# A hybrid attention block on one core: the last head's mix tiles without memory, and another order at the head's end

## The chip, the cores and the metric

The kernel runs on one core of a Trainium2 chip. The metric is the device time of one execution in microseconds (us). The engines are called PE (TensorE), ACT (ScalarE), DVE (VectorE), POOL (GpSimd) and SP (SyncE, which here only issues DMAs). Each runs its own instruction stream in program order and waits on semaphores.

## The reference, cut to what matters

One row of 1024 tokens with 1024 features, float32. The input is normalised and projected by one matrix into the queries, keys, values and gates of three head groups: A (sliding window with sinks), B (differential attention) and M (attention to 256 memory tokens).

```python
proj = rmsnorm(x, g_norm) @ w_in                      # 1024 x 4352
b_out = rmsnorm(b_heads, b_subln_g) * (1.0 - lam_init)
gated = concatenate([a_out * silu(ag), b_out * silu(bg), m_out * silu(mg)])
y = rmsnorm(x + gated @ w_out, g_final)               # w_out 1536 x 1024
```

## The kernel before, in words

**Numbers.** Every large matrix product is made of three float32r products: each operand is split into a high part (a rounding copy, made on ACT: w_hi, p_hi, mix_hi, wo hi) and a low part (the rest, raw minus high: w_lo, p_lo, mix_lo, wo lo). So a projection or an output product is three matmuls (lines 1282 to 1284).

**Heads.** A loop runs four times, once for each head. In a head, PE projects eight weight tiles w = 0..7 in two halves s (512 tokens each), and each half in four quarters q of six matmuls. Tile 7 is the B gate. Between the quarters, PE does the attention pieces that the table `BETWEEN[(w, s, q)]` names. All engines walk the same list `HEAD`; for each step each of them does its own part, in list order. An `evacuate(w, s)` step follows the last quarter of a half and comes ahead of the pieces that BETWEEN names there. PE takes nothing out of order: if the piece after a quarter must wait, all later quarters wait too.

**The pieces that the change touches**, for head h:
- `b_squares(s)`: the row sums for B's norm. POOL squares b_out (L856) and later subtracts (L859), ACT copies the high part between the two (L709), PE multiplies by ones (L1509, L1510), DVE scales the result (L1183). ACT's copy goes to a slot of p_hi, a ring of two slots that the steps b_spread, m_spread and b_squares use in list order (`PT_AT`); it waits until the user two places back has been consumed by PE (`p_slot_free`).
- `b_finish(s)`: ACT takes a square root (L715), DVE a reciprocal of 128x512 (L1189) and a product into b_out (L1191).
- `b_gate`: DVE multiplies b_out into the B gate, two halves (L1199). It needs both b_finish and the evacuated gate (L1056).
- `a_spread(3)`, `a_mix(3)`: PE transposes probabilities (L1489), DVE copies them (L1175), PE multiplies by the values (L1500), DVE gates the result (L1116). `m_spread`, `m_mix` are the same for M; the mix output has one bank (mixo), so each mix waits until DVE's gate (L1116) of the one before has read it (o_free).
- `m_norm(m)`: ACT takes the exponentials (L693, L695), DVE a reciprocal (L1137), POOL a product (L836).

**The tail.** `mixed` in device memory holds 12 tiles of 128 rows x 1024 tokens, three for each head. Each head spills its three gate buffers there, and after the heads they come back as mix_raw by row tiles of 128 tokens. The last head's tiles 9 to 11 make that trip at the end of the heads (`spill(g, H)`, `load_mix(.., 1)`). ACT makes mix_hi and the high parts of the output weights wo 1..11, POOL makes mix_lo and the low parts of wo 1 and 2 (`POOL_WO`), DVE those of wo 3 to 11 and one piece of mix_lo. PE's output products then run over eight row tiles x two halves x 12 tiles; for the first pair of row tiles it goes j = 0..6 for all four outputs, and then j = 7..11 one output at a time, because these weights come last. Weights 4 to 11 lie over the normalised input, so they are loaded when the last projection is done.

Of the kernel before, what the change touches and what calls it, by code (L numbers as in the profile page):

```python
# [20 lines left out]
F32 = mybir.dt.float32  # L21
F32R = mybir.dt.float32r
ALU = mybir.AluOpType
# [3 lines left out]
P = 128  # L27
# [6 lines left out]
HEADS = 4  # L34
DK = 64
AQ, AK, AV, AG, BQ, BK, BV, BG, MQ, MG = 0, 512, 640, 768, 1280, 1792, 2304, 2816, 3328, 3840
MIX_TILES = 12
POOL_WO = 2
LAM_INIT = 0.8 - 0.6
# [42 lines left out]
    (7, 0, 1): [("a_mix", 2), ("m_norm", 3), ("m_spread", 2)],  # L82
    (7, 0, 2): [("m_mix", 1)],
    (7, 0, 3): [("m_spread", 3), ("m_mix", 2)],
    (7, 1, 0): [("a_spread", 3), ("m_mix", 3), ("b_squares", 1)],
    (7, 1, 1): [("b_finish", 0)],
    (7, 1, 2): [("b_finish", 1)],
    (7, 1, 3): [("b_gate",), ("a_mix", 3)],
}
# [73 lines left out]
def build(nc, x, mem, w_in, g_norm, a_sinks, lq1, lk1, lq2, lk2, subln_g, g_mem, w_mem_kv, w_out,  # L163
          g_final, y):
    mixed = nc.dram_tensor("mixed", (MIX_TILES * P, SEQ), F32).ap()

# [24 lines left out]
    with ctx:  # L191
        def sem(name):
# [5 lines left out]
        w_lo = sb("w_lo", [P, 2, KT * P], F32R)  # L198
        gates = {g: sb(f"gate_{g}", [P, SEQ]) for g in "abm"}
        ident = sb("ident", [P, P])  # L200
# [79 lines left out]
        MIX = MIX_TILES * P * 4  # L280
        spread_end = begins["mk_raw"] + 2 * HEADS * MEM * 4
        mix_raw = [sb_over("mix_raw0", [P, MIX_TILES, P], spread_end - MIX, spread_end),
                   sb_over("mix_raw1", [P, MIX_TILES, P], begins["b_bias"], main_end)]
        mix_hi = [sb_over("mix_hi0", [P, MIX_TILES, P], main_end, nc.sbuf_usable_end, F32R),
# [76 lines left out]
        mix_full = [sem("mix_full0"), sem("mix_full1")]  # L361
        mix_last = [sem("mix_last0"), sem("mix_last1")]
        wo_full = [sem(f"wo_full{j}") for j in range(1, MIX_TILES)]
        wo_hi_done = sem("wo_hi_done")
        wo_lo_first = sem("wo_lo_first")
        wo_lo_done = sem("wo_lo_done")
# [26 lines left out]
        def _(sp):  # L393
# [75 lines left out]

            def load_mix(par, t, part):  # L470

                js, done = ((slice(0, 9), mix_full), (slice(9, 12), mix_last))[part]
                sp.dma_start(mix_raw[par][:, js, :], mixed_v[:, js, bass.ds(t * P, P)]).then_inc(done[par], 16)

# [8 lines left out]
            sp.wait_ge(mkv_lo, 2 * HEADS)  # L483
            load_mix(0, 0, 0)
# [3 lines left out]
            load_mix(1, 1, 0)  # L488
            sp.wait_ge(s_full, NS * HEADS)
# [3 lines left out]
            sp.wait_ge(acc_full, PRE_ACC + 2 * NT * HEADS)  # L493
            for j in range(4, 8):
                load_wo(j)
            for g in "mab":
                spill(g, H)
            load_wo(8)
            load_wo(9)
            for g in "mab":  # L500
                sp.wait_ge(spilled[g], 16 * HEADS)
            load_mix(0, 0, 1)
            load_mix(1, 1, 1)
            for j in range(10, MIX_TILES):
                load_wo(j)
# [15 lines left out]
            def next_pair(z, split):  # L521

                for par in range(2):
                    sp.wait_ge(mix_lo_done, split[par])
                    for part in range(2):
                        load_mix(par, z * 2 + (par + 2), part)
# [5 lines left out]
            sp.wait_ge(mix_lo_mid, 1)  # L532
            next_pair(0, (4, 5))
            with sp.Fori(0, ST // 2 - 2) as n:
                next_pair(n + 1, (n * 4 + 7, n * 4 + 9))
            for par in range(2):
# [6 lines left out]
        def _(act):  # L543
# [195 lines left out]

            def mix_hi_part(par, js, arrived, full):  # L740
                act.wait_ge(arrived[par], full)
                act.activation(mix_hi[par][:, js, :], mix_raw[par][:, js, :], ACT.Copy).then_inc(mix_hi_done, 1)  # L742

            def wo_hi_part(j):
                act.wait_ge(wo_full[j - 1], 32)
                act.activation(wo[j - 1][:, 0, :], wo_raw[j - 1][:, :], ACT.Copy).then_inc(wo_hi_done, 1)

            mix_hi_part(0, slice(0, 3), mix_full, 16)
            act.wait_ge(t_full, at(T_AT[("b_spread", 3, 3)], HEADS - 1, NTB, PRE_T))
            mix_hi_part(1, slice(0, 3), mix_full, 16)  # L750
            wo_hi_part(1)
            wo_hi_part(2)
            mix_hi_part(0, slice(3, 9), mix_full, 16)
            mix_hi_part(1, slice(3, 9), mix_full, 16)
# [18 lines left out]
            with act.Fori(0, ST // 2 - 1) as z:  # L773
                for par in range(2):

                    act.wait_ge(y_full, z * 4 + 2 * (par + 1))
                    mix_hi_part(par, slice(0, 9), mix_full, z * 16 + 32)
                    mix_hi_part(par, slice(9, 12), mix_last, z * 16 + 32)
                    finish_row(par, z)
# [5 lines left out]
        def _(pool):  # L785
# [91 lines left out]
            def mix_lo_part(par, js, n):  # L877
# [3 lines left out]
                                   ALU.subtract).then_inc(mix_lo_done, 1)  # L881

            pool.wait_ge(pt_done, NMIX * HEADS)
            pool.wait_ge(t_full, PRE_T + NTB * HEADS)
            for par in range(2):
                mix_lo_part(par, slice(0, 3), par)
            for j in range(1, POOL_WO + 1):
                pool.wait_ge(wo_hi_done, j)
                pool.tensor_tensor(wo[j - 1][:, 1, :], wo_raw[j - 1][:, :], wo[j - 1][:, 0, :].bitcast(F32),
                                   ALU.subtract).then_inc(wo_lo_first, 1)  # L890
            mix_lo_part(1, slice(3, 9), 3)
            for par in range(2):
                mix_lo_part(par, slice(9, 12), 4 + par)
            with pool.Fori(0, ST // 2 - 1) as z:
                for par in range(2):
                    for p, js in enumerate((slice(0, 9), slice(9, 12))):
                        mix_lo_part(par, js, z * 4 + (6 + 2 * par + p))


        @block.vector  # L900
        def _(dve):
# [106 lines left out]
            with dve.Fori(0, HEADS) as h:  # L1008
# [194 lines left out]
                for s in HEAD:  # L1203
# [40 lines left out]
            dve.tensor_tensor(mix_lo[0][:, 3:9, :], mix_raw[0][:, 3:9, :], mix_hi[0][:, 3:9, :].bitcast(F32),  # L1244
                              ALU.subtract).then_inc(mix_lo_mid, 1)
# [33 lines left out]
        def _(pe):  # L1279
# [269 lines left out]
            def w_out_ready(j):  # L1549
                if j == 0:  # L1550
                    pe.wait_ge(w_lo_done, PRE_TILES + NT * HEADS + 1)
                elif j <= POOL_WO:
                    pe.wait_ge(wo_lo_first, j)
                else:
                    pe.wait_ge(wo_lo_done, j - POOL_WO)

# [4 lines left out]
            for j in range(7):  # L1561
                w_out_ready(j)
                for par in range(2):
                    if j == 0:
                        pe.wait_ge(mix_lo_done, 1 + par)
                    if j == 3:
                        pe.wait_ge(*((mix_lo_done, 3) if par else (mix_lo_mid, 1)))
                    for s in range(2):
                        y_product(par, s, j)
            for par in range(2):  # L1570
                pe.wait_ge(mix_lo_done, 4 + par)
                for s in range(2):
                    for j in range(7, MIX_TILES):
                        w_out_ready(j)
                        last = y_product(par, s, j)
                    last.then_inc(y_full, 1)
            with pe.Fori(0, ST // 2 - 1) as z:
                for par in range(2):
                    pe.wait_ge(mix_lo_done, z * 4 + (7 + 2 * par))
# [27 lines left out]
```

## Time and profile before

| | us |
|---|---|
| median of 3 runs | 776.75 |
| lowest and highest run | 775.76, 778.9 |
| the profiled execution: span from first to last instruction | 775.9 |
| PE busy in it | 755.9 (97%) |
| DVE, ACT, POOL busy | 433.7, 321.7, 236.4 |

The profiled execution has no separate time of its own beside its span of 775.9 us; what lies around the span is in the 0.85 us up to the median. Times in the rows are microseconds from the start of the span. Matmul ends are modelled: of two dense matmuls the second starts 0.23 us after the first although each is shown 0.39 us long.

### The profile page before, as it was taken

The page shows a single profiled execution, that of the slowest core. Times are in us where ns is not written, and L with a number is a line of the kernel's source. Part 1 is how long each engine was busy: PE and PEld are TensorE (multiplying, and loading weights), DVE is VectorE, ACT ScalarE, POOL GpSimd, SP SyncE. Part 2 cuts the span into 40 slices and gives each one's busy share as a digit, 9 for nine tenths or more (in the row PEclk, how much of TensorE's full clock was granted, in tenths as well). Part 3 has the DMA queues.
Part 4 walks back from the last instruction along what each step waited for, and adds up shares of the span by engine and source line. Part 5 has one row for each costly group of instructions (what it writes and reads, how often), then busy time and mean ns, then how long its engine had stood idle before and what let it go on. Part 6 is the DMA issues. An engine that isn't in the chain of part 4 may idle for free.

```text
span 775.9 us, 12264 instructions
## 1 busy us (share of the span) xinstructions
PE 755.9 (97%) x3908; PEld 596.3 (77%) x3908; DVE 433.7 (56%) x915; ACT 321.7 (41%) x727; POOL 236.4 (30%) x204
## 2 busy tenths in 40 slices
PE   7999999999999999999999999999999988999996
PEld 7887877778877777887777688877768866888885
DVE  5875235666763566677346666734666695422231
ACT  5761323444542344454334444433444472421220
POOL 3663212224422222442322244222224451311110
PEclk9999999999999999999999999999999999999998
DMA  7662120011042001103300110240011359554111
GB/s 251 209 171 55 28 54 29 28 28 29 1 136 54 27 27 27 27 0 121 70 27 27 27 27 0 91 100 27 27 41 44 85 135 279 162 150 124 65 54 54
DMA packets 83155, 56.61 MB, mean 73 GB/s; under 512 B 36400, under 2 KB 75312, under 8 KB 83120
## 3 DMA queue, kind: packets, MB, share of 16 engines
q1 hardware_dynamic: 83120, 56.25, 26.0%
q8 instruction: 10, 0.16, 0.1%
q14 instruction: 25, 0.20, 0.1%
HBM read 45.75 MB, written 10.49 MB: 72 GB/s over the span
## 4 chain that ended last, share of the span: by engine, by line
PE 88%; issue 4%; DVE 2%; POOL 2%; DMA 2%; SPq 1%; ACT 0%; DVEq 0%; POOLq 0%
PE acc L1282 17%; PE acc L1284 16%; PE acc L1283 16%; PE score L1403 5%; PE score L1401 4%; PE score L1282 3%; PE score L1283 3%; PE score L1284 3%; PE trans L1422 2%; PE trans L1282 2%; PE trans L1284 2%; PE trans L1283 2%; POOL w_lo L803 2%; PE mixo L1282 2%; PE score L1479 2%
## 5 line engine op out<-in xcount | busy, mean ns | idle before, releaser
L1282 PE MATMUL acc<-x_hi,w_hi 128*128 128x512 f32 x544 | 221.4, 407 | 0.2 <-POOL w_lo L803 0.2
L1283 PE MATMUL acc<-x_lo,w_hi 128*128 128x512 f32 x544 | 214.6, 395 | 0.0
L1284 PE MATMUL acc<-x_hi,w_lo 128*128 128x512 f32 x544 | 214.6, 394 | 0.0
L803 POOL TENSOR_TENSOR w_lo<-w_raw,w_hi 128x512 fp32r<-128x512 f32 x86 | 114.1, 1348 | 205.5 <-ACT w_hi L548 205.5
L1282 PEld LDWEIGHTS acc<-x_hi,w_hi 128*128 128x128 f32 x544 | 102.1, 188 | 27.6 <-issue 5.7
L1284 PEld LDWEIGHTS acc<-x_hi,w_lo 128*128 128x128 f32 x544 | 102.0, 188 | 24.9
L1283 PEld LDWEIGHTS acc<-x_lo,w_hi 128*128 128x128 f32 x544 | 102.2, 188 | 20.0
L1077 DVE CUSTOM_DVE_ANT_0 logits<-score,b_bias 128x512 f32<-128x512 f32 (+1 forms) x96 | 57.2, 602 | 44.6 <-PE score L1403 34.9
L653 ACT ACTIVATE logits<-logits,stats_b 128x256 f32<-128x256 f32 (+3 forms) x64 | 52.7, 825 | 68.7 <-DVE stats_b L1085 68.7
L662 ACT ACTIVATE p_hi<-trans 128x512 fp32r<-128x512 f32 x56 | 32.6, 596 | 74.2 <-PE trans L1422 44.1
L548 ACT ACTIVATE w_hi<-w_raw 128x512 fp32r<-128x512 f32 x86 | 49.4, 624 | 26.2 <-PE acc L1284 20.4
L830 POOL TENSOR_SCALAR logits<-logits,stats_b,small 128x256 f32<-128x256 f32 (+3 forms) x32 | 28.3, 883 | 104.2 <-DVE stats_b L1094 104.2
L1104 DVE TENSOR_TENSOR p_lo<-trans,p_hi 128x512 fp32r<-128x512 f32 x56 | 37.9, 689 | 31.4 <-ACT p_hi L662 31.0
L880 POOL TENSOR_TENSOR mix_lo<-mix_raw,mix_hi 128x384 fp32r<-128x384 f32 (+2 forms) x17 | 28.2, 1677 | 85.4 <-ACT mix_hi L742 85.4
L1097 DVE SCALAR_TENSOR_TENSOR logits<-logits,stats_b 128x256 f32<-128x256 f32 (+3 forms) x32 | 28.3, 885 | 38.0 <-POOL logits L830 38.0
L701 ACT ACTIVATE a_band<-a_band,stats_a 128x128 f32<-128x128 f32 x64 | 25.0, 393 | 58.1 <-DVE stats_a L1162 58.1
L1403 PE MATMUL score<-k_lo,q_b 64*128 64x512 f32 (+1 forms) x96 | 43.9, 457 | 0.0
L1401 PE MATMUL score<-k_b,q_b 128*128 128x512 f32 (+1 forms) x96 | 40.1, 418 | 0.0
L1282 PE MATMUL score<-wo,mix_hi 128*128 128x512 f32 x88 | 35.4, 403 | 4.1 <-DVE wo L1248 3.8
L1403 PEld LDWEIGHTS score<-k_lo,q_b 64*128 64x128 f32 x96 | 17.5, 183 | 22.9 <-issue 20.3
L1283 PE MATMUL score<-wo,mix_hi 128*128 128x512 f32 x88 | 34.8, 395 | 0.0
L1284 PE MATMUL score<-wo,mix_lo 128*128 128x512 f32 x88 | 34.8, 395 | 0.0
(193 smaller groups left out, 1333.7 us busy)
## 6 DMA issues: line engine op xcount, KB each, us to landing
w_raw<-in_w_in SPq DMA_DIRECT2D x68, 256.0 KB, 3.4
wo_raw<-in_w_out SPq DMA_DIRECT2D x22, 256.0 KB, 5.6
mix_raw<-mixed SPq DMA_DIRECT2D x8, 576.0 KB, 5.8
w_raw<-in_w_mem_kv SPq DMA_DIRECT2D x16, 256.0 KB, 3.9
logits<-in_x SPq DMA_DIRECT2D x8, 512.0 KB, 4.5
x_res<-in_x SPq DMA_DIRECT2D x8, 512.0 KB, 3.3
out_y<-y_row SPq DMA_DIRECT2D x16, 256.0 KB, 2.1
mixed<-gate_a SPq DMA_DIRECT2D x4, 512.0 KB, 3.1
```

The lines of the kernel that those rows point to most:

```text
L548: act.activation(w_hi[:, slot, cols], w_raw[:, slot, cols], ACT.Copy).then_inc(w_hi_done, 1)
L653: act.activation(logits[:, i % 2, c, 0:width], logits[:, i % 2, c, 0:width], ACT.Exp, bias=b_neg[:, 2 * (i % 2) + c:2 * (i % 2) + c + 1], ...
L662: act.activation(out, trans[:, bank, :], ACT.Copy).then_inc(t_hi, 1)
L803: last = pool.tensor_tensor(w_lo[:, slot, cols], w_raw[:, slot, cols], w_hi[:, slot, cols].bitcast(F32), ALU.subtract)
L830: pool.tensor_scalar(logits[:, i % 2, 1, 0:width], logits[:, i % 2, 1, 0:width], b_inv[:, 2 * (i % 2) + 1:2 * (i % 2) + 2], neg_lam, ALU.m ...
L1077: dve.tensor_tensor_reduce(out=logits[:, i % 2, c, a:a + n], in0=score[:, unit % S_RING, 0:n], in1=b_bias[:, rel:rel + n], scale=1.0, scal ...
L1104: dve.tensor_tensor(out, trans[:, T_AT[step] % T_RING, :], hi.bitcast(F32), ALU.subtract)\
L1282: pe.matmul(out, a_hi, b_hi, start=start, stop=False, skip_group_check=True)
L1283: pe.matmul(out, a_hi, b_lo, start=False, stop=False, skip_group_check=True)
L1284: return pe.matmul(out, a_lo, b_hi, start=False, stop=stop, skip_group_check=True)
L1401: pe.matmul(out, q_b[:, c, rows_i], k_b[:, c, a:a + n], start=True, stop=False, skip_group_check=True)
L1403: pe.matmul(out, q_b[ps, c, rows_i], k_lo[ps, a:a + n], start=False, stop=True, skip_group_check=True).then_inc(s_full, 1)
```

## The change

1. The last head's mix tiles (9 to 11) are split into mix_hi and mix_lo straight from the gate buffers on chip, for every row tile. Their spill and the loads of that part go away; `mixed` has nine tiles.
2. All eleven low output weights are made by DVE; POOL makes none. DVE also makes both middle pieces of mix_lo, after wo 2.
3. In every head: b_squares(1) moves from after the quarter (7,1,0) to after (7,0,2); b_finish(0) from (7,1,1) to (7,0,3); b_finish(1) from (7,1,2) to (7,1,1); a_mix(3) from after (7,1,3) to after (7,1,2), and so ahead of the evacuation of the last half and of b_gate.
4. After the last projection SP issues weights 4 to 11 in one row, with no spill or load between.

```diff
-POOL_WO = 2
+SPILL_TILES = 9
-    (7, 0, 2): [("m_mix", 1)],
-    (7, 0, 3): [("m_spread", 3), ("m_mix", 2)],
-    (7, 1, 0): [("a_spread", 3), ("m_mix", 3), ("b_squares", 1)],
-    (7, 1, 1): [("b_finish", 0)],
-    (7, 1, 2): [("b_finish", 1)],
-    (7, 1, 3): [("b_gate",), ("a_mix", 3)],
+    (7, 0, 2): [("m_mix", 1), ("b_squares", 1)],
+    (7, 0, 3): [("m_spread", 3), ("m_mix", 2), ("b_finish", 0)],
+    (7, 1, 0): [("a_spread", 3), ("m_mix", 3)],
+    (7, 1, 1): [("b_finish", 1)],
+    (7, 1, 2): [("a_mix", 3)],
+    (7, 1, 3): [("b_gate",)],
...
-            for j in range(4, 8):
-                load_wo(j)
-            for g in "mab":
-                spill(g, H)
-            load_wo(8)
-            load_wo(9)
-            for g in "mab":
-                sp.wait_ge(spilled[g], 16 * HEADS)
-            load_mix(0, 0, 1)
-            load_mix(1, 1, 1)
-            for j in range(10, MIX_TILES):
+            for j in range(4, MIX_TILES):
                 load_wo(j)
...
+            def gates_hi_part(par, t):
+                act.activation(mix_hi[par][:, SPILL_TILES:MIX_TILES, :], gate_rows[:, :, bass.ds(t * P, P)], ACT.Copy)\
+                   .then_inc(mix_hi_done, 1)
...
-            mix_hi_part(0, slice(9, 12), mix_last, 16)
-            mix_hi_part(1, slice(9, 12), mix_last, 16)
+            act.wait_ge(o_free, NO * HEADS)
+            act.wait_ge(b_gated, 2 * HEADS)
+            gates_hi_part(0, 0)
+            gates_hi_part(1, 1)
...
+            def gates_lo_part(par, t, n):
+
+                pool.wait_ge(mix_hi_done, n + 1)
+                js = slice(SPILL_TILES, MIX_TILES)
+                pool.tensor_tensor(mix_lo[par][:, js, :], gate_rows[:, :, bass.ds(t * P, P)],
+                                   mix_hi[par][:, js, :].bitcast(F32), ALU.subtract).then_inc(mix_lo_done, 1)
...
-            for j in range(1, POOL_WO + 1):
-                pool.wait_ge(wo_hi_done, j)
-                pool.tensor_tensor(wo[j - 1][:, 1, :], wo_raw[j - 1][:, :], wo[j - 1][:, 0, :].bitcast(F32),
-                                   ALU.subtract).then_inc(wo_lo_first, 1)
-            mix_lo_part(1, slice(3, 9), 3)
             for par in range(2):
-                mix_lo_part(par, slice(9, 12), 4 + par)
+                gates_lo_part(par, par, 4 + par)
...
-            dve.wait_ge(mix_hi_done, 3)
...
-            for j in range(POOL_WO + 1, MIX_TILES):
+            for j in range(1, MIX_TILES):
                 dve.wait_ge(wo_hi_done, j)
                 dve.tensor_tensor(wo[j - 1][:, 1, :], wo_raw[j - 1][:, :],
                                   wo[j - 1][:, 0, :].bitcast(F32), ALU.subtract).then_inc(wo_lo_done, 1)
+                if j == 2:
+                    for par in range(2):
+                        dve.wait_ge(mix_hi_done, 3 + par)
+                        dve.tensor_tensor(mix_lo[par][:, 3:9, :], mix_raw[par][:, 3:9, :],
+                                          mix_hi[par][:, 3:9, :].bitcast(F32), ALU.subtract).then_inc(mix_lo_mid, 1)
```

## Rows read from the trace of the kernel before

**Rows 1.** Timeline of PE, last head, tile 7: start us, us, engine, line, operation.

```profile
618.25 0.28 PE L1284 MATMUL mixo<-p_hi,mv_lo 128*128 128x256 f32 x1
618.37 0.39 PE L1282 MATMUL acc<-x_hi,w_hi 128*128 128x512 f32 x1
...
620.79 0.28 PE L1284 MATMUL mixo<-p_hi,mv_lo 128*128 128x256 f32 x1
...
622.67 0.36 PE L1282 MATMUL mixo<-p_hi,mv_hi 128*128 128x256 f32 x1
...
623.46 0.39 PE L1509 MATMUL trans<-p_hi,ones 128*128 128x512 f32 x1
```

**Rows 2.** Timeline of ACT in the same stretch.

```profile
616.45 0.47 ACT L693 ACTIVATE m_probs<-score,stats_m 128x256 f32<-128x256 f32 x1 [2.24 <-PE trans L1458]
...
621.10 0.63 ACT L709 ACTIVATE p_hi<-logits 128x512 fp32r<-128x512 f32 x1
621.75 1.28 ACT L715 ACT_TABLE_LOAD   x1
623.05 0.64 ACT L715 ACTIVATE logits<-logits 128x512 f32<-128x512 f32 x1
```

**Rows 3.** Timeline of POOL in the same stretch.

```profile
617.75 1.04 POOL L836 TENSOR_TENSOR m_probs<-m_probs,stats_m 128x512 f32<-128x512 f32 x1 [1.25 <-DVE stats_m L1137]
618.75 1.04 POOL L856 TENSOR_TENSOR logits<-b_out 128x512 f32<-128x512 f32 x1
621.81 1.28 POOL L859 TENSOR_TENSOR p_lo<-logits,p_hi 128x512 fp32r<-128x512 f32 x1 [2.02 <-ACT p_hi L709]
```

**Rows 4.** Timeline of DVE, last head's end.

```profile
621.20 0.68 DVE L1104 TENSOR_TENSOR p_lo<-trans,p_hi 128x512 fp32r<-128x512 f32 x1
621.80 0.42 DVE L1116 SCALAR_TENSOR_TENSOR gate_m<-mixo,gate_m 128x256 f32<-128x256 f32 x1
622.95 0.69 DVE L1175 COPY a_pt<-trans 128x512 f32<-128x512 f32 x1 [0.73 <-PE trans L1489]
...
624.73 3.34 DVE L1189 RECIPROCAL logits<-logits 128x512 f32<-128x512 f32 x1
628.11 0.69 DVE L1191 TENSOR_TENSOR b_out<-b_out,logits 128x512 f32<-128x512 f32 x1
...
632.10 2.30 DVE L1191 TENSOR_TENSOR b_out<-b_out,logits 128x512 f32<-128x512 f32 x1
```

**Rows 5.** Timeline of POOL near the end of the head before.

```profile
481.14 1.04 POOL L856 TENSOR_TENSOR logits<-b_out 128x512 f32<-128x512 f32 x1
```

**Rows 6.** Timeline of ACT and PE, from the last projection on.

```profile
628.22 0.69 PE L1500 MATMUL mixo<-a_pt,a_v 128*64 128x64 f32 x16
...
628.33 0.60 ACT L645 ACTIVATE gate_b<-acc 128x512 f32<-128x512 f32 x1 [1.54 <-PE acc L1284]
...
630.64 0.47 PE L1282 MATMUL score<-w_hi,mix_hi 128*128 128x512 f32 x1 [1.74 <-POOL mix_lo L880]
```

**Rows 7.** Timeline of PE in the tail.

```profile
641.86 0.59 PE L1282 MATMUL score<-wo,mix_hi 128*128 128x512 f32 x1 [2.13 <-DVE wo L1248]
...
645.61 0.39 PE L1282 MATMUL trans<-wo,mix_hi 128*128 128x512 f32 x1
```

**Rows 8.** Windows: us, PE, PEld, DVE, ACT, POOL busy (instructions), PEclk, DMA, GB/s.

```profile
630.00:640.00 10.00, 8.86 (x36) 6.52 (x36) 9.97 (x7) 7.14 (x8) 8.92 (x5) 1.00 1.03 254
643.00:644.00 1.00, 1.00 (x4) 0.71 (x4) 1.00 (x2) 0.00 (x0) 0.00 (x0) 0.50 0.70 209
```

**Rows 9.** Timeline of PE in the prologue.

```profile
13.58 1.62 PE L1290 MATMUL trans<-ident,logits 128*128 128x128 f32 x8 [2.40 <-DVE k_b L940]
```

**Rows 10.** The chain that ended last, in the tail.

```profile
687.84 0.23 PE trans L1282
...
769.48 0.24 PE trans L1284
```

**Rows 11.** Line 1248, DVE's low output weights.

```profile
L1248 DVE TENSOR_TENSOR wo<-wo_raw,wo x9: 1211/1221/1226, 640.6 to 659.0; 128x1024 fp32r<-128x1024 f32 x9
```

More of the change, by code:

```diff
@@ L164, in build @@
           g_final, y):
-    mixed = nc.dram_tensor("mixed", (MIX_TILES * P, SEQ), F32).ap()
+    mixed = nc.dram_tensor("mixed", (SPILL_TILES * P, SEQ), F32).ap()
     x_rows = x.rearrange("b (t p) d -> p (b t) d", p=P)
@@ L198, in build @@
         w_lo = sb("w_lo", [P, 2, KT * P], F32R)
-        gates = {g: sb(f"gate_{g}", [P, SEQ]) for g in "abm"}
+        gate_rows = sb("gates", [P, 3, SEQ])
+        gates = {g: gate_rows[:, n, :] for n, g in enumerate("abm")}
         ident = sb("ident", [P, P])
@@ L280, in build @@
         MIX = MIX_TILES * P * 4
+        MIX_RAW = SPILL_TILES * P * 4
         spread_end = begins["mk_raw"] + 2 * HEADS * MEM * 4
-        mix_raw = [sb_over("mix_raw0", [P, MIX_TILES, P], spread_end - MIX, spread_end),
-                   sb_over("mix_raw1", [P, MIX_TILES, P], begins["b_bias"], main_end)]
+        mix_raw = [sb_over("mix_raw0", [P, SPILL_TILES, P], spread_end - MIX_RAW, spread_end),
+                   sb_over("mix_raw1", [P, SPILL_TILES, P], begins["b_bias"], main_end)]
         mix_hi = [sb_over("mix_hi0", [P, MIX_TILES, P], main_end, nc.sbuf_usable_end, F32R),
@@ L361, in build @@
         mix_full = [sem("mix_full0"), sem("mix_full1")]
-        mix_last = [sem("mix_last0"), sem("mix_last1")]
         wo_full = [sem(f"wo_full{j}") for j in range(1, MIX_TILES)]
         wo_hi_done = sem("wo_hi_done")
-        wo_lo_first = sem("wo_lo_first")
         wo_lo_done = sem("wo_lo_done")
@@ L468, in load_wo, with load_mix @@
                       .then_inc(wo_full[j - 1] if j else raw_full[0], 16)
-            def load_mix(par, t, part):
-                js, done = ((slice(0, 9), mix_full), (slice(9, 12), mix_last))[part]
-                sp.dma_start(mix_raw[par][:, js, :], mixed_v[:, js, bass.ds(t * P, P)]).then_inc(done[par], 16)
+            def load_mix(par, t):
+                sp.dma_start(mix_raw[par][:, :, :], mixed_v[:, :, bass.ds(t * P, P)]).then_inc(mix_full[par], 16)
             def load_residual(par, t):
@@ L483, in _ @@
             sp.wait_ge(mkv_lo, 2 * HEADS)
-            load_mix(0, 0, 0)
+            load_mix(0, 0)
             sp.wait_ge(s_full, at(S_AT[("b", 7, 1, 1)], H, NS))
@@ L487, in _ @@
             sp.wait_ge(s_free_dve, len(S_BY_DVE) * HEADS)
-            load_mix(1, 1, 0)
+            load_mix(1, 1)
             sp.wait_ge(s_full, NS * HEADS)
@@ L524, in next_pair @@
                     sp.wait_ge(mix_lo_done, split[par])
-                    for part in range(2):
-                        load_mix(par, z * 2 + (par + 2), part)
+                    load_mix(par, z * 2 + (par + 2))
                 for par in range(2):
@@ L530, in next_pair @@
                     store(par, z)
-            sp.wait_ge(mix_lo_mid, 1)
-            next_pair(0, (4, 5))
+            sp.wait_ge(mix_lo_mid, 2)
+            next_pair(0, (1, 2))
             with sp.Fori(0, ST // 2 - 2) as n:
-                next_pair(n + 1, (n * 4 + 7, n * 4 + 9))
+                next_pair(n + 1, (n * 4 + 5, n * 4 + 7))
             for par in range(2):
@@ L737, in _, with mix_hi_part @@
                         b_finish(s[1])
-            def mix_hi_part(par, js, arrived, full):
-                act.wait_ge(arrived[par], full)
+            def mix_hi_part(par, js, full):
+                act.wait_ge(mix_full[par], full)
                 act.activation(mix_hi[par][:, js, :], mix_raw[par][:, js, :], ACT.Copy).then_inc(mix_hi_done, 1)
+            def gates_hi_part(par, t):
+                act.activation(mix_hi[par][:, SPILL_TILES:MIX_TILES, :], gate_rows[:, :, bass.ds(t * P, P)], ACT.Copy)\
+                   .then_inc(mix_hi_done, 1)
             def wo_hi_part(j):
@@ L746, in wo_hi_part @@
                 act.activation(wo[j - 1][:, 0, :], wo_raw[j - 1][:, :], ACT.Copy).then_inc(wo_hi_done, 1)
-            mix_hi_part(0, slice(0, 3), mix_full, 16)
+            mix_hi_part(0, slice(0, 3), 16)
             act.wait_ge(t_full, at(T_AT[("b_spread", 3, 3)], HEADS - 1, NTB, PRE_T))
-            mix_hi_part(1, slice(0, 3), mix_full, 16)
+            mix_hi_part(1, slice(0, 3), 16)
             wo_hi_part(1)
             wo_hi_part(2)
-            mix_hi_part(0, slice(3, 9), mix_full, 16)
-            mix_hi_part(1, slice(3, 9), mix_full, 16)
+            mix_hi_part(0, slice(3, 9), 16)
+            mix_hi_part(1, slice(3, 9), 16)
             for j in range(3, 7):
                 wo_hi_part(j)
-            mix_hi_part(0, slice(9, 12), mix_last, 16)
-            mix_hi_part(1, slice(9, 12), mix_last, 16)
+            act.wait_ge(o_free, NO * HEADS)
+            act.wait_ge(b_gated, 2 * HEADS)
+            gates_hi_part(0, 0)
+            gates_hi_part(1, 1)
             for j in range(7, MIX_TILES):
@@ L776, in _ @@
                     act.wait_ge(y_full, z * 4 + 2 * (par + 1))
-                    mix_hi_part(par, slice(0, 9), mix_full, z * 16 + 32)
-                    mix_hi_part(par, slice(9, 12), mix_last, z * 16 + 32)
+                    mix_hi_part(par, slice(0, 9), z * 16 + 32)
+                    gates_hi_part(par, z * 2 + (par + 2))
                     finish_row(par, z)
@@ L886, in _ @@
                 mix_lo_part(par, slice(0, 3), par)
-            for j in range(1, POOL_WO + 1):
-                pool.wait_ge(wo_hi_done, j)
-                pool.tensor_tensor(wo[j - 1][:, 1, :], wo_raw[j - 1][:, :], wo[j - 1][:, 0, :].bitcast(F32),
-                                   ALU.subtract).then_inc(wo_lo_first, 1)
-            mix_lo_part(1, slice(3, 9), 3)
             for par in range(2):
-                mix_lo_part(par, slice(9, 12), 4 + par)
+                gates_lo_part(par, par, 4 + par)
             with pool.Fori(0, ST // 2 - 1) as z:
                 for par in range(2):
-                    for p, js in enumerate((slice(0, 9), slice(9, 12))):
-                        mix_lo_part(par, js, z * 4 + (6 + 2 * par + p))
+                    mix_lo_part(par, slice(0, 9), z * 4 + (6 + 2 * par))
+                    gates_lo_part(par, z * 2 + (par + 2), z * 4 + (7 + 2 * par))
         @block.vector
@@ L1239, in _ @@
                         b_gate()
-            dve.wait_ge(mix_hi_done, 3)
             dve.wait_ge(pt_done, NMIX * HEADS)
             dve.wait_ge(t_full, PRE_T + NTB * HEADS)
-            dve.tensor_tensor(mix_lo[0][:, 3:9, :], mix_raw[0][:, 3:9, :], mix_hi[0][:, 3:9, :].bitcast(F32),
-                              ALU.subtract).then_inc(mix_lo_mid, 1)
-            for j in range(POOL_WO + 1, MIX_TILES):
+            for j in range(1, MIX_TILES):
                 dve.wait_ge(wo_hi_done, j)
@@ L1551, in w_out_ready @@
                     pe.wait_ge(w_lo_done, PRE_TILES + NT * HEADS + 1)
-                elif j <= POOL_WO:
-                    pe.wait_ge(wo_lo_first, j)
                 else:
-                    pe.wait_ge(wo_lo_done, j - POOL_WO)
+                    pe.wait_ge(wo_lo_done, j)
             pe.wait_ge(t_free, PRE_T + NTB * HEADS)
@@ L1566, in _ @@
                     if j == 3:
-                        pe.wait_ge(*((mix_lo_done, 3) if par else (mix_lo_mid, 1)))
+                        pe.wait_ge(mix_lo_mid, 1 + par)
                     for s in range(2):
@@ L1570, in _ @@
             for par in range(2):
-                pe.wait_ge(mix_lo_done, 4 + par)
+                pe.wait_ge(mix_lo_done, 3 + par)
                 for s in range(2):
@@ L1578, in _ @@
                 for par in range(2):
-                    pe.wait_ge(mix_lo_done, z * 4 + (7 + 2 * par))
+                    pe.wait_ge(mix_lo_done, z * 4 + (6 + 2 * par))
                     for s in range(2):
```

## The prediction

> **What bounds the kernel now.** I read the page first: the span is 775.9 us (in the table above, with the page's busy times), and PE is busy for 97% of it. So only what makes PE wait, or what lets it wait less, moves the time. Then I read the timelines of the four engines at the end of the last head and in the tail. Through the end of a head PE never stops: its matmuls follow each other 0.23 us (512 columns) or 0.12 us (256 columns) apart [rows 1]. In the tail it does stop. The chain of the tail has PE from 687.84 to 769.48 + 0.24, which is 81.9 us for ten of the sixteen output units, 8.19 us each [rows 10]. Sixteen would be 131.0 us, but the first output product starts at 630.64 [rows 6] and the last ends at 769.7, 139.1 us. So 8.0 us of the tail are waits and a slow clock. That is all that parts 1, 2 and 4 of the change can win there.
>
> **The head's end, step by step.** I take the last head's times; the others have the same pattern (POOL's square of b_out stands at 618.75 here and at 481.14 one head earlier, one head period apart) [rows 3, 5].
>
> First wait: b_squares(1) now follows m_mix(1) directly. PE would issue it at 618.37, where the next quarter starts now [rows 1]. Its operands come by a chain that doesn't get earlier: m_spread(2) frees m_probs, ACT's exponentials of m_norm(3) start at 616.45 [rows 2], POOL's product follows at 617.75 and POOL's square, behind it in POOL's order, at 618.75 for 1.04 us, to 619.8 [rows 3]. Then ACT's high copy, 0.63 [rows 2], and POOL's subtraction, 1.28 [rows 3], with about 0.05 to 0.15 between engines: 0.08 is what lies between 621.10 + 0.63 and 621.81. So PE can start at 619.79 + 0.06 + 0.63 + 0.08 + 1.28 + 0.15 = 621.99. It waits 3.6 us. Before, ACT's copy came at 621.10, POOL ended at 623.09, and PE asked for it at 623.46 [rows 1 to 3]: the quarter, a_spread(3) and m_mix(3) covered the chain. In the new order nothing covers it, and everything behind it in PE's queue waits too.
>
> Second wait, small: b_squares takes two matmuls, 0.46. The quarter (7,0,3) starts at 622.45, and the last matmul of m_mix(2) at 622.45 + 2.42 = 624.87 (618.37 to 620.79 before [rows 1]), ending at 625.15. With b_squares(1) ahead of it in the ring, the user of p_hi two places before m_spread(3) is m_spread(2) now, not m_spread(1). So ACT's copy for m_spread(3), which ran ahead of m_mix(2) before, waits for the end of m_mix(2), and behind it on ACT wait the table load and the square root. Copy (0.6, as in L709) to 625.8, DVE's low part and gate (0.1 + 0.6 + 0.42 with the spacing of [rows 4]) to 626.85. PE wants m_mix(3) 1.88 after the last matmul of m_mix(2) [rows 1], at 626.75: 0.2 us of wait.
>
> Third wait: b_finish(0) now stands on DVE ahead of the copy for a_spread(3) and of the gate of m_mix(3), and PE's a_mix(3) needs both. ACT: copy to 625.77, table load and square root 1.96 (621.75 to 623.05 + 0.64) to 627.73 [rows 2]. DVE: reciprocal from 627.78, product 3.38 later, copy 0.61 later, gate 0.71 later, 0.42 long (624.73 to 628.11 and the durations beside it) [rows 4]: 632.9. PE is ready for a_mix(3) at 626.94 + 0.79 (622.67 to 623.46 [rows 1]) + twelve matmuls 2.8 + 0.1 = 630.6, and starts at 633.0: 2.4 us.
>
> The second square root needs no new table and is long done; the second reciprocal comes only behind the gate of m_mix(3), so a_mix(3) doesn't wait for it.
>
> Together 3.6 + 0.2 + 2.4 = 6.2 us in each head. After the first three heads nothing gives it back, since PE has no wait there now: 18.6 us. The next head's evacuations don't suffer: DVE is done with b_gate 5 us after PE starts the next head, before the first half of it ends at 24 x 0.23 = 5.6 us.
>
> At this place a rule of the Trainium skill speaks for more. The row shows the table load with 1.28 us, the square root 0.02 behind it, and the copy before it ended 0.02 ahead [rows 2]. "ScalarE: Activation LUTs", section "What ACT_TABLE_LOAD costs", adds a drain of 1.38 us to each load, 2.66 in all. By that the third wait would be 1.4 longer in each head. The row shows no such drain.
>
> SP issues the spills of heads 0 to 2 behind the moved gates; the waits of its queue lie beside 137.6 us of head (618.75 - 481.14), and what it loads next is needed one tile later, 11 us of PE, so I cost that at nothing.
>
> **The last head and the tail.** Parts 1 and 4: the spills and the late loads go. PE's (7,1,3) is issued by 633.0 + 0.61 + 1.40 = 635.0. ACT's tanh stands 0.2 behind it, and the first output product 2.31 behind that (628.33 to 630.64 [rows 6]): 637.5, against 630.64, so 6.9 late; a_mix no longer fills that gap. Weights 4 to 11 are eight tiles of 512 KB. At the 254 GB/s of the window 630 to 640, where the queue is full [rows 8], they take 16.5 us, to about 654; PE wants tile 11 some 96 matmuls x 0.23 = 22 us after its start, at 659.6. That is cover of some 5 us, so the DMA queue and ACT (idle otherwise) cost nothing; without that cover it would be 2.1 us for a tile. The gates' splits on ACT and POOL replace equal ones from mix_raw. DVE: its second reciprocal runs 632.9 to 636.3, then 0.69, the gate of A, the last evacuation and two products of b_gate. These have two inputs in SBUF, as the one of L1191 that took 2.30 beside POOL's wo work instead of 0.69 [rows 4]; now POOL has only the two small mix_lo pieces, so I give them 0.4 us of waiting and DVE is free near 639.7. Low weight 1 takes 1.22 [rows 11], to 640.9, and PE wants it at 640.4: a wait of 0.7. All later ones come at 1.2 or less on DVE against 2.8 us of PE for each j. So of the 8.0 us of loss about 0.4 + 0.7 stay: 6.9 - 8.0 + 1.1 = 0.0. The tail pays for its own late start and no more.
>
> **The clock.** At 641.86, after 2.13 us of waiting, the matmuls take 0.63 and the window behind has a granted clock of 0.50 (1.2 GHz) [rows 7, 8]; the same shows behind a 2.40 wait in the prologue, where eight transposes take 1.62 [rows 9]. The wait of 1.74 at 630.64 did no such thing [rows 6]. The first of these cost 1.7 us: the nine matmuls that start from 641.86 on, up to the one at 645.61 [rows 7], take 3.75 us, and dense ones 9 x 0.23 = 2.07. The new kernel has four waits of 3.6, four of 2.4 and one of 2.3. None falling gives 0, all nine give 15.3. I take five to six, 9 us, as every 3.6 should do it, and the others in part.
>
> **The sum.** 776.75 + 18.6 + 0.0 + 9 = 804. The span of 775.9 belongs to an execution at the median or just below it (0.85 apart), so the difference goes onto the median.
>
> **Rivals.**
> - Only the first wait is real, and the reciprocals are hidden: 3 x 3.8, the tail 2.4 better, the clock 4 x 1.7: 776.75 + 11.4 - 2.4 + 6.8 = 793. For it: a_mix(3) has 12 matmuls of cover. Against: the DVE chain is 7.8 us long. Chance 0.05.
> - Faster: PE finds b_squares(1) ready. It decides at 618.37: if POOL's subtraction has ended by then, the reciprocals start 3 to 4 us earlier too, no head waits, and only the tail counts, 0.6 - 8.0 + 1.1 = -6.3: 770.4. Against: POOL's square starts only at 618.75 [rows 3]. Chance 0.05.
> - The third wait is longer by the drain that the Trainium skill's ScalarE page gives: 4 x 1.4 more, 776.75 + 18.6 + 5.5 + 9 = 810. The row of the table load speaks against it: chance 0.02.
> - The tail fails: weights 4 to 11 come in slower than 2.8 us a tile, or DVE's eleven low weights become the bound. Two tiles late, 4 us: 808. Chance 0.03.
>
> **How the numbers follow.** The forecast has 0.85. Its range is 776.75 + 18.6 = 795 without any fall of the clock and 811 with all nine; with 1 us for the engine spacings, and reaching to the first rival, 793 to 813. Less than 0.5% (3.9 us) is about what a measurement here can't tell from no change. Faster: the second rival, 0.05. Same: a part of the waits hidden by something that I don't see and the tail's gain against the rest, 0.02. Slower 0.93.
>
> **What would show it.** In each head a wait of PE for POOL L859 of some 3.6 us ahead of b_squares(1), and one for DVE L1116 or L1175 of some 2.4 ahead of the last a_mix; a head period 6 to 9 us longer; first output product some 2.3 us behind tanh; no waits of PE on wo after the first; PEclk below 1 at the heads' ends. The prediction is wrong if PE shows no wait ahead of b_squares(1), or if the clock stays at 1.00 there (then 795).

## The result and the profile after

The changed kernel takes 807.69 us (median of 4 runs, 803.77 to 808.52) against 776.52: a ratio of 1.0385, 95% interval 1.0361 to 1.0408. It is slower by 31 us. The forecast was 804, 793 to 813. In the runs with both on record the time is 1.75 to 1.95 us above the span. So the profile of the kernel before, with its span of 775.9, is of an execution of about 777.7, 1.2 above the median, and the spans differ by 29.7 where the medians differ by 31.2.

The page of the kernel after, its head and the two rows of shares over time:

```profile
span 805.6 us, 12254 instructions
...
PE 764.2 (95%) x3908; PEld 602.9 (75%) x3908; DVE 434.9 (54%) x918; ACT 321.6 (40%) x727; POOL 232.9 (29%) x201
...
PE   6899999999799999988999998899999969999996
...
PEclk9999999999999999989999999999999988999999
```

PE had been busy for 97% of a span of 775.9. A slice is 20.1 us. PE's row has its dips where the heads end (slices 11, 18 and 19, 25 and 26, 33, counted from 1; those at 2 and 40 are the prologue and the end), and the clock's row is 8 at the second head's end (18) and at the last one's (33 and 34). It stays at 9 elsewhere: the third head's slow stretch (501.03 to some 507) lies across two slices, and the first head's is short (210.1 to 213.6).

Who PE waited for in the kernel after (us in total, times, longest):

```profile
PE trans L1507 <- POOL p_lo L853: 13.9, 4, 3.5
PE mixo L1498 <- DVE gates L1112: 8.6, 4, 2.2
...
PE score L1280 <- POOL mix_lo L874: 2.4, 1, 2.4
```

The first two are new: four times 3.5 us in front of b_squares(1) (now L1507), four times 2.2 in front of a_mix(3) (now L1498). The waits for the output weights, 3.8 us in five parts in the kernel before, are gone from the list. In the timeline of PE, head 1 of the kernel after:

```profile
350.77 0.28 PE L1282 MATMUL mixo<-p_hi,mv_lo 128*128 128x256 f32 x1
354.53 0.76 PE L1507 MATMUL trans<-p_hi,ones 128*128 128x512 f32 x1 [3.49 <-POOL p_lo L853]
355.10 0.63 PE L1508 MATMUL trans<-p_lo,ones 128*128 128x512 f32 x1
...
368.25 0.69 PE L1498 MATMUL mixo<-a_pt,a_v 128*64 128x64 f32 x16 [2.16 <-DVE gates L1112]
```

Compare [rows 1], where the last matmul of m_mix(1) at 618.25 is followed 0.12 us later by the next quarter. Here 3.76 us lie between. Behind the gap matmuls start 0.43 us apart; a window of it (columns as in [rows 8]) has the granted clock at 0.50, that is the lower of its two levels, 1.2 GHz:

```profile
355.00:356.00 1.00, 1.00 (x4) 0.71 (x3) 0.24 (x1) 0.00 (x0) 0.00 (x0) 0.50 0.00 0
```

The chain that the prediction wrote down stands in the timelines of POOL and ACT at the last head's end, kernel after:

```profile
643.27 1.04 POOL L830 TENSOR_TENSOR m_probs<-m_probs,stats_m 128x512 f32<-128x512 f32 x1 [1.26 <-DVE stats_m L1133]
644.26 1.04 POOL L850 TENSOR_TENSOR logits<-b_out 128x512 f32<-128x512 f32 x1
646.12 1.26 POOL L853 TENSOR_TENSOR p_lo<-logits,p_hi 128x512 fp32r<-128x512 f32 x1 [0.82 <-ACT p_hi L697]
```

```profile
645.42 0.63 ACT L697 ACTIVATE p_hi<-logits 128x512 fp32r<-128x512 f32 x1 [1.94 <-POOL logits L850]
...
652.27 0.60 ACT L650 ACTIVATE p_hi<-trans 128x512 fp32r<-128x512 f32 x1 [0.63 <-PE mixo L1282]
652.89 1.28 ACT L703 ACT_TABLE_LOAD   x1
654.18 1.15 ACT L703 ACTIVATE logits<-logits 128x512 f32<-128x512 f32 x2
```

Product, square, ACT's copy, POOL's subtraction, one behind the other, with 0.1 us between engines. Each of them waits for the one before. The second fence also has the head of the second chain: ACT's copy for m_spread(3) waits for m_mix(2), then the table, then the square roots. And on DVE, in the kernel after, the first reciprocal stands in front of the copy and the gate that PE needs (before they came first, [rows 4]):

```profile
654.85 3.35 DVE L1185 RECIPROCAL logits<-logits 128x512 f32<-128x512 f32 x1 [0.93 <-ACT logits L703]
658.23 0.69 DVE L1187 TENSOR_TENSOR b_out<-b_out,logits 128x512 f32<-128x512 f32 x1
658.84 0.68 DVE L1171 COPY a_pt<-trans 128x512 f32<-128x512 f32 x1
659.45 0.41 DVE L1112 SCALAR_TENSOR_TENSOR gates<-mixo,gates 128x256 f32<-128x256 f32 x1
```

The span grew by 29.7 us. b_squares(1) starts at 209.10, 354.53, 501.03 and 647.53 in the four heads: periods of 145.4, 146.5 and 146.5 against 137.6 before, 25.6 in three heads. The other 4.1 are the fourth head's end and the tail taken together: the first output product comes at 665.77 instead of 630.64, and from there to the end of the last one it takes 133.7 us instead of 139.1.

### The profile page after: what moved, and what is told of

The parts are those of the page before. It is cut to its first block, busy times and chain, and to the rows that moved or that the text cites. A ratio compares the mean times of both kernels' runs of the same rounds, so it can differ in the third digit from the quotient of the medians.

```text
span 805.6 us, 12254 instructions
## 1 busy us (share of the span) xinstructions
PE 764.2 (95%) x3908; PEld 602.9 (75%) x3908; DVE 434.9 (54%) x918; ACT 321.6 (40%) x727; POOL 232.9 (29%) x201
## 4 chain that ended last, share of the span: by engine, by line
PE 81%; issue 6%; POOL 5%; DVE 4%; ACT 2%; DMA 1%; SPq 0%; DVEq 0%; POOLq 0%; ACTq 0%
PE acc L1280 15%; PE acc L1282 14%; PE acc L1281 14%; PE score L1401 5%; PE score L1399 4%; PE score L1280 3%; POOL w_lo L797 3%; PE score L1282 3%; PE score L1281 3%; PE trans L1280 3%; PE trans L1281 3%; PE trans L1282 3%; PE trans L1420 2%; PE score L1477 2%; DVE logits L1185 2%
## 5 line engine op out<-in xcount | busy, mean ns | idle before, releaser
L1280 PE MATMUL acc<-x_hi,w_hi 128*128 128x512 f32 x544 | 223.8, 411 | 0.5 <-POOL w_lo L797 0.5
L874 POOL TENSOR_TENSOR mix_lo<-mix_raw,mix_hi 128x1152 fp32r<-128x1152 f32 (+1 forms) x8 | 18.5, 2317 | 88.0 <-ACT mix_hi L730 88.0
L1280 PE MATMUL trans<-wo,mix_hi 128*128 128x512 f32 x88 | 34.3, 390 | 0.0
```

The lines of the kernel that those rows point to most:

```text
L1280: pe.matmul(out, a_hi, b_hi, start=start, stop=False, skip_group_check=True)
```

## The experiments

Each kernel is an edit of the changed kernel or of the one before, and its ratio is to the kernel before, run beside it on the same chip. e1 to e4 ran on one chip, e5 to e8 on a second, e9 and e10 on a third, and the kernel before had medians of 777.63, 777.78 and 776.87 there, so differences between medians of different chips are good to about 1 us only.

**e1: b_squares(1) alone put back.**

```diff
-    (7, 0, 2): [("m_mix", 1), ("b_squares", 1)],
+    (7, 0, 2): [("m_mix", 1)],
...
-    (7, 1, 0): [("a_spread", 3), ("m_mix", 3)],
+    (7, 1, 0): [("a_spread", 3), ("m_mix", 3), ("b_squares", 1)],
```

> The changed kernel with b_squares(1) back behind m_mix(3) in (7,1,0); all else as changed. Two-waits theory: the wait of 3.5 us at b_squares(1) in each head becomes about 1.6 (ACT's high copy now stands behind the table load and the square root of b_finish(0)), a_mix(3) no longer waits because PE arrives later than the gate of m_mix(3), and the clock stays up in the heads: three heads x 1.6 = 4.8, the tail 4 us better than before: 777, with up to two drops of the clock 780. Rival, that the early b_finish(0) alone costs about as much as b_squares(1): 790 or more.

777.87 us, ratio 0.9999 (0.9986 to 1.0013). Its list of what PE waited for:

```profile
PE trans L1507 <- POOL p_lo L853: 5.5, 4, 1.4
```

No wait for DVE in front of a_mix(3) any more, and a head period of 139.2 (b_squares(1) at 351.54 and 490.75): 1.6 us longer than before, as expected. One step put back in place wins 30 us, and what it leaves is just eaten up by the better tail.

**e2: b_finish(0) and (1) alone put back.**

```diff
-    (7, 0, 3): [("m_spread", 3), ("m_mix", 2), ("b_finish", 0)],
+    (7, 0, 3): [("m_spread", 3), ("m_mix", 2)],
...
-    (7, 1, 1): [("b_finish", 1)],
-    (7, 1, 2): [("a_mix", 3)],
+    (7, 1, 1): [("b_finish", 0)],
+    (7, 1, 2): [("b_finish", 1), ("a_mix", 3)],
```

> The changed kernel with b_finish(0) and b_finish(1) back in (7,1,1) and (7,1,2), b_squares(1) still behind m_mix(1). Two-waits theory: the wait at b_squares(1) stays at 3.5 us with its slow clock (2 to 2.8 us a head), the wait of a_mix(3) goes: three heads x 6 = 18, the tail about 1 us better than before: 792 to 796. Rival, that b_squares(1) is the single cause and the other wait only follows from it: 805 to 808, as the changed kernel.

797.58 us, ratio 1.0243 (1.0202 to 1.0285); 1.6 above the range given. The wait in front of b_squares(1) is as long as in the changed kernel and the one in front of a_mix(3) is gone:

```profile
PE trans L1507 <- POOL p_lo L853: 13.9, 4, 3.5
PE score L1280 <- POOL mix_lo L874: 2.4, 1, 2.4
```

So there are two separate causes: 10 to 11 us of the 31 (by the medians and by the ratios) hang on the two b_finish steps and go without touching b_squares(1). They were moved together; that it is b_finish(0) is read from DVE's rows above, where its reciprocal and product alone stand ahead of the copy and the gate. The two parts don't simply add up. In e1, ACT's copy for m_spread(3) is not held by m_mix(2), so DVE's first reciprocal starts at 627.99, 2 us ahead of b_squares(1) at 629.97, and a_mix(3) finds its operands ready.

**e3: the tail of the changed kernel, the head's end as before.** The six lines of BETWEEN are those of the kernel before.

> The changed kernel with the order of the head's end as before; only the tail differs (gates split on chip, all low weights on VectorE, weights 4 to 11 in one row). Two-waits theory: heads as before with no wait of PE, the tail loses 3.3 us instead of 8 (0.4 at the first product, 2.9 at j = 1, because DVE reaches the low weights late), 772, with one drop of the clock 773.5. Rival, that the change of the tail itself costs time (DMA in one row, gates' splits, DVE as the bound): 777 or more.

772.82 us, ratio 0.9948 (0.9929 to 0.9966). The new tail is a gain of 4.0 us by the ratio. Its profile is of its slowest run (776.75). It shows the wait that is left at j = 1, and the slow clock behind it:

```profile
638.84 0.79 PE L1280 MATMUL score<-wo,mix_hi 128*128 128x512 f32 x1 [2.56 <-DVE wo L1241]
639.43 0.63 PE L1281 MATMUL score<-wo,mix_hi 128*128 128x512 f32 x1
```

**e4: the new order in the kernel before, the old tail.** Only BETWEEN is changed.

> The kernel before with only the new order of the head's end; the tail goes through memory as before. Two-waits theory: the same waits of 3.5 and 2.2 us in each head as the changed kernel, and the old tail's last gap partly hidden since its first output product comes late: 805 to 812. Rival, that the loss is in the new tail: 777 to 790.

814.08 us, ratio 1.0477 (1.0441 to 1.0513): the highest of all, and 2 us above the range given. Its list has the same two waits, 13.9 and 8.6 us, and the old tail's trip through memory still costs a gap at j = 7:

```profile
690.27 0.47 PE L1282 MATMUL score<-wo,mix_hi 128*128 128x512 f32 x1 [2.42 <-DVE wo L1248]
```

e3 and e4 together are the change: 0.9948 x 1.0477 = 1.0423, against 1.0385 measured. The order of the head's end is the whole loss. Behind it the new tail is worth more than in e3, 0.9% instead of 0.5%. The old tail's gap at j = 7 was 1.14 us in the kernel before and is 2.42 here.

**e5: the waits filled with dummy work.** The question was what the slow clock adds to the waits.

```diff
+                    if s == 1:
+                        for _ in range(30):
+                            pe.transpose(out[:, 0:P], ident[:, :], ident[:, :])
                     pe.wait_ge(squares_split, at(s, h, 2))
...
+                    if m == 3:
+                        for _ in range(18):
+                            pe.transpose(trans[:, T_AT[("m_spread", 3)] % T_RING, 0:P], ident[:, :], ident[:, :])
                     out = o_bank(("a_mix", m))
```

> The changed kernel with dummy transposes on PE inside its two waits: 30 ahead of b_squares(1), 18 ahead of a_mix(3), into a bank that is free then, 0.11 us each, so that they end before the waits do. The waits themselves keep their length. Theory that the slow clock adds to the waits: the granted clock stays at 1.00 in the heads, a head's period falls from 146.5 to 143.6 or so, and only the wait at the first output product can still slow the clock: 795 to 799. Rival, that the clock is an accompaniment that costs nothing since PE waits anyway: 806 to 809, as the changed kernel.

796.07 us, ratio 1.0235 (1.0208 to 1.0261). There is more work on PE, and the time is 11.6 us below the changed kernel. The window over head 1, first of the kernel after, then of e5:

```profile
330.00:470.00 140.00, 134.33 (x684) 102.94 (x682) 79.02 (x172) 56.73 (x133) 40.84 (x38) 0.98 0.14 38
```

```profile
330.00:470.00 140.00, 139.61 (x745) 108.19 (x745) 82.04 (x180) 56.62 (x134) 40.62 (x37) 1.00 0.15 41
```

And a_mix(3) in two heads of e5, 143.83 us apart:

```profile
364.09 0.69 PE L1501 MATMUL mixo<-a_pt,a_v 128*64 128x64 f32 x16 [0.20 <-DVE gates L1112]
...
507.92 0.69 PE L1501 MATMUL mixo<-a_pt,a_v 128*64 128x64 f32 x16 [0.20 <-DVE gates L1112]
```

At a full clock a head is 143.8 - 137.6 = 6.2 us longer. That is the waits alone: the dummies did not lengthen them, since b_squares(1) starts 3.69 behind the last matmul of m_mix(1) (349.29 to 352.98) and 3.76 without them. The fourth head and the first output product of e5:

```profile
640.63 0.50 PE L1513 MATMUL trans<-p_hi,ones 128*128 128x512 f32 x1
...
656.60 0.47 PE L1280 MATMUL score<-w_hi,mix_hi 128*128 128x512 f32 x1 [2.58 <-POOL mix_lo L874]
...
659.84 0.50 PE L1280 MATMUL score<-wo,mix_hi 128*128 128x512 f32 x1 [0.20 <-DVE wo L1241]
```

**e6: POOL's square early.** Only POOL's order is changed: the square for b_squares(1) ahead of the product of m_norm(3).

```diff
                 def m_norm(m):
+                    if m == 3:
+                        b_square_made(1)
                     pool.wait_ge(m_inv_made, at(m, h, 4))
...
```

> The changed kernel with POOL's square for b_squares(1) ahead of its product of m_norm(3) instead of behind it. The theory names the chain that makes the first wait (POOL's m_norm(3) product, POOL's square, ACT's copy, POOL's subtraction). With the square made early, the copy waits for m_mix(1) alone (end of it 0.3 us behind the asking), then 0.63 + 0.08 + 1.28 + 0.15: the wait at b_squares(1) falls from 3.5 to 2.3 us, the one of a_mix(3) stays at 2.2: 4.8 us less in four heads, with less of the slow clock 797 to 803. Rival, that the two-slot ring of p_hi sets the wait, not POOL's order: it stays at 3.5, 807.

798.92 us, ratio 1.026 (1.0237 to 1.0283). The two lines of its list:

```profile
PE mixo L1505 <- DVE gates L1119: 8.6, 4, 2.2
PE trans L1514 <- POOL p_lo L860: 8.6, 4, 2.1
```

The first wait falls from 3.5 to 2.1, the second stays. So POOL's order sets the length of the first wait as the prediction had it, down to where the ring takes over: ACT's copy now starts at 642.39, right behind the end of m_mix(1) (642.07 + 0.28).

**e7 and e10: POOL makes one low weight again.** From e3; e10 is the same kernel once more, beside e9.

```diff
+            pool.wait_ge(wo_hi_done, 1)
+            pool.tensor_tensor(wo[0][:, 1, :], wo_raw[0][:, :], wo[0][:, 0, :].bitcast(F32),
+                               ALU.subtract).then_inc(wo_lo_first, 1)
...
-            for j in range(1, MIX_TILES):
+            for j in range(2, MIX_TILES):
...
-                if j == 2:
-                    for par in range(2):
-                        dve.wait_ge(mix_hi_done, 3 + par)
+                if j in (2, 3):
+                    par = j - 2
+                    dve.wait_ge(mix_hi_done, 3 + par)
...
```

> The tail-only kernel (head's end as before) with two edits: POOL makes the low part of weight 1 again, and DVE makes weight 3 between its two pieces of mix_lo. The tail-only kernel waits 2.6 us for DVE's weight 1 and has a slow clock behind it. If DVE's late arrival is the bound of the new tail: a wait of 0.4 at j = 1 and 1.1 at j = 2, no slow clock, 2 to 3 us below the tail-only kernel: 770. If POOL's work slows DVE's products by more than it saves: 773 or more.

> The kernel of e7 once more, beside e9 on the same chip: 771.6 as before, since nothing is changed in it. A theory that e7's gain over the kernel before came from that chip or call expects a ratio nearer to 1 than 0.9916.

771.61 us, ratio 0.9916 (0.9894 to 0.9937), and 771.36, ratio 0.9932 (0.9918 to 0.9946). It is faster than the kernel before by 0.7 to 0.8%. Against e3 it is 1.2 to 1.5 us by the medians and 1.2 to 2.5 by the ratios, where 2 to 3 was expected, and the intervals of the ratios overlap, so that gain is not settled. e3's wait of 2.56 is gone, but in the profile of e7 (an execution of 774.03) the clock fell behind the wait of the first output product instead:

```profile
633.12 0.54 PE L1284 MATMUL score<-w_hi,mix_hi 128*128 128x512 f32 x1 [1.74 <-POOL mix_lo L875]
633.46 0.63 PE L1285 MATMUL score<-w_lo,mix_hi 128*128 128x512 f32 x1
```

**e8: only the gates' tiles split on chip.** Tail of e3 with the low weights made as before (POOL 1 and 2, DVE 3 to 11).

```diff
+            for j in range(1, 3):
+                pool.wait_ge(wo_hi_done, j)
+                pool.tensor_tensor(wo[j - 1][:, 1, :], wo_raw[j - 1][:, :], wo[j - 1][:, 0, :].bitcast(F32),
+                                   ALU.subtract).then_inc(wo_lo_first, 1)
+            mix_lo_part(1, slice(3, 9), 3)
...
```

> Only part 1 of the change (the last head's tiles split from the gate buffers on chip, weights 4 to 11 in one row); the head's end and who makes which low weight as before. By the account of the tail: the gap of 1.3 us at j = 7 and the four of 0.4 behind it go, the wait of 2.1 at j = 3 and the slow clock behind it stay: 3.1 to 3.4 us below the kernel before, 773 to 774. Rival, that the move of the low weights to DVE brings a good part of the tail's gain: 776.

774.99 us, ratio 0.996 (0.9943 to 0.9977): 1 us above the range given. Rows of its timelines of DVE and of POOL show why DVE is late there:

```profile
634.78 4.57 DVE L1201 SCALAR_TENSOR_TENSOR gates<-b_out,small,gates 128x512 f32<-128x512 f32 x2
```

```profile
633.65 2.88 POOL L891 TENSOR_TENSOR wo<-wo_raw,wo 128x1024 fp32r<-128x1024 f32 x1
636.47 2.32 POOL L875 TENSOR_TENSOR mix_lo<-mix_raw,mix_hi 128x768 fp32r<-128x768 f32 x1
640.31 3.04 POOL L882 TENSOR_TENSOR mix_lo<-gates,mix_hi 128x384 fp32r<-128x384 f32 x2 [1.52 <-ACT mix_hi L734]
```

The same two products of b_gate take 1.40 in e7, where POOL is idle by then, and 4.55 in the kernel before, which has the same low weights on POOL. And with the gates' split at 640.31, DVE's next weight is late too. It takes 2.02 instead of the 1.21 of [rows 11]:

```profile
640.47 2.02 DVE L1250 TENSOR_TENSOR wo<-wo_raw,wo 128x1024 fp32r<-128x1024 f32 x1
```

PE's wait at j = 3 is 2.93, longer by the same 0.8 than the 2.13 of [rows 7].

**e9: dummies in two waits of e7** (14 transposes in front of the first output product, 28 instead of 12 in the prologue).

```diff
-BUSY = (32, 12, 16)
+BUSY = (32, 28, 16)
...
+            for _ in range(14):
+                pe.transpose(score[:, 2, 0:P], ident[:, :], ident[:, :])
             for j in range(7):
```

> The kernel of e7 with dummy transposes inside two waits of PE that are left: 14 behind the last projection (wait of 1.7 us for the first mix_lo) and 16 more in the prologue (28 instead of 12, ahead of a wait of 2.4). In the profile of e7 the clock fell behind the 1.7 wait and cost 1.6 us there, and once more in the prologue. If the slow clock behind these waits is a real part of what is left: 1.5 to 3 us below e7 on the same chip, 769 to 770, and a narrower spread of the runs. Rival, that the dummies delay the real work or change nothing: within 0.5 us of e7 or above it.

770.33 us, ratio 0.9925 (0.9907 to 0.9943), beside e10 with 0.9932 on the same chip. The median is 1 us lower, 0.3 above the range given, and the intervals overlap: not settled. Five of its six runs lie within 0.6 us (770.10 to 770.70), the sixth is 774.35; those of e10 go from 769.71 to 773.06. In e10's profiled execution, its fastest, the clock stood at 1.00 behind the same wait of 1.74 without any dummies.

## Why the prediction was right

**The first wait.** Forecast 3.6 in each head, by adding five durations from other places of the trace. The timeline has 3.76 between the last start of m_mix(1) and b_squares(1), that is 3.64 more than dense, and a listed wait of 3.49. e6 shows that it is this chain.

**The small wait.** Forecast 0.2 on m_mix(3). In e5, at a full clock, m_mix(3) starts 0.66 behind a_spread(3) (357.49 to 358.15), against 0.36 before (622.31 to 622.67): 0.3. One reading behind it was loose: before, ACT's copy for m_spread(3) ran beside m_mix(2) (620.46, and m_mix(2) from 620.12), not ahead of it.

**The wait of a_mix(3).** Forecast 2.4, listed 2.16. e2 shows that it hangs on the early b_finish steps, and DVE's rows that it is b_finish(0).

**The sum of the waits.** Forecast 6.2 us a head. In e5, where the clock stays up, a head is 6.2 us longer. And nothing gives it back: all three heads keep it.

**The tail.** Forecast 0.0 at a full clock, made of 6.9 late at the first output product and 6.9 less behind it. e5 has it at a full clock. From the last b_squares(1) to the first output product are 15.97 us (640.63 to 656.60) where the prediction had 15.5 (621.99 to 637.5): 0.5 more, half of it because the product starts 2.55 behind tanh and not 2.31. From there to the end of the last product are 131.7 (656.60 to 787.89 + 0.39) where it had 131.0 + 1.1: 0.4 less, since the wait for weight 1 is 0.20 and not 0.7. That these two misses cancel is luck. The span of e5 is 18.5 above the one before: three times 6.2, and nothing for the tail. In the changed kernel the same two stretches are 18.2 (647.53 to 665.77) and 133.7, so 2.3 and 2.0 more are slow clock. Twelve slow matmuls at the start (665.77 to 671.02, 5.25 against 2.8) cost 2.4; against that the wait for weight 1, which makes the next matmul in e5 0.4 late (659.24 to 659.84, 0.60 instead of 0.23), does not show.

**The clock.** This is the term of the sum that was mis-sized. Forecast 9 us, between 0 and 15.3. e5 measures 11.6 in the medians and 11.2 in the spans (805.6 - 794.4). By stretches it is 1.6, 2.7 and 2.7 in the first three head periods (7.8, 8.9, 8.9 less 6.2), then the 2.3 and 2.0 above: 11.3 with the rounding. The number of falls was near, five to six of nine. The clock fell behind all four waits of 3.5 and behind one of 2.2, and there it stayed at 0.50 from 661 to 671, through the wait for the first output product too. Their cost was off: a slow stretch behind a wait of 3.5 costs up to 2.7, not 1.7, because it lasts longer (from 354.53 to 360.2). Of the four waits of 2.2 in front of a_mix(3) only that one let the clock fall.

**The sum.** 18.6 + 0.0 + 9 was forecast. In the spans it was 29.7, with 11.2 of clock and 18.5 of waits and tail. The rest of the 3 us by which the time came out above 804 is the base. The prediction took the span of 775.9 for an execution at the median or just below it, and it was about 1 us above the 776.75 that the sum starts from: 777.7 + 18.5 + 11.2 = 807.4, the profiled execution of the changed kernel (807.38).

**Cover of the weights' loads.** It held, but with less to spare. The last weight's high part starts on ACT at 684.50, 21 us after SP began to issue, not 16.5, and PE asks for it 3.3 us after DVE's part is done (690.13, 686.81), where the forecast had 5 us to spare. ACT waited 7.2 us for these loads in all; nobody waited for ACT but DVE.

**The rivals.** That only the first wait is real fell with e2 and with the list of waits. That PE finds b_squares(1) ready fell at once. That the tail fails fell with e3. For the third one, ACT's table load with a drain: "ScalarE: Activation LUTs", section "What ACT_TABLE_LOAD costs", of the Trainium skill gives 2.66 us in all, and the rows above have 652.89 + 1.28 = 654.17 and the square root at 654.18. No drain shows here either.

## What to carry to other kernels

When a step is moved forward on an engine that is the bound and runs in order, add up the chain that feeds it from its first part that can't move, on every engine and in that engine's own order, a short ring's slots included: the chain here was forecast at 5.5 us (616.45 to 621.99), and PE had 1.9 us of work left beside it (616.45 to 618.37). A long operation (a reciprocal of 3.3 us) put ahead of a short one that the bound engine needs becomes a wait of the bound engine, here 2.2 us in each of four heads. And look at each part of a change alone: here the tail alone won 4 us and the order alone cost 37, and the tail without the order, a little reworked, was the fastest of all (771.4 to 771.6, and 770.3 with dummies).

## What the runs showed that I had not expected

- Whether TensorE's clock falls behind a wait can't be told from the wait's length alone. It stood at 1.00 behind the 2.16 us in front of a_mix(3) in three heads and was 0.69 (window 660 to 662) behind the same 2.16 in the fourth. It fell behind 2.13 us in the kernel before [rows 7], 2.56 in e3 and 1.74 in e7, and not behind 2.58 in e5 nor behind 1.74 in [rows 6]. e7 and e10 are the same kernel with the same wait of 1.74: it fell in the one profile and not in the other.
- The fall need not come at once. Behind the wait of 2.93 in e8 the first matmuls are dense, and from 644.09 on, 1.6 us after it, they start 0.43 us apart for 3.4 us:

```profile
642.53 0.50 PE L1284 MATMUL score<-wo,mix_hi 128*128 128x512 f32 x1 [2.93 <-DVE wo L1250]
642.87 0.39 PE L1285 MATMUL score<-wo,mix_hi 128*128 128x512 f32 x1
...
644.09 0.63 PE L1284 MATMUL trans<-wo,mix_hi 128*128 128x512 f32 x1
644.52 0.63 PE L1285 MATMUL trans<-wo,mix_hi 128*128 128x512 f32 x1
```

- These falls may have a share in the spread of the runs, which no run here shows by itself. The prologue alone has waits of 1.1 to 2.5 us, and the kernel before ran from 775.1 to 780.0 over all its runs.
- DVE's products with two inputs in SBUF take longer beside a POOL instruction: 2.30 instead of 0.69 for one [rows 4], 4.57 instead of 1.40 for two (e8, e7). The Trainium skill says in "SBUF — State Buffer", section "Who interferes with whom", that a DVE instruction with two SBUF inputs contends with a GpSimd instruction that reads SBUF, and the runs agree. That a split on chip instead of through memory can by this make the next wait longer (2.13 to 2.93 in e8) was new to me.
- What stays open: how much of e9's 1 us is real, and what decides in which execution the clock falls.
